# FFN gate and up projections: one 512-column product for the high weights, with the two sums in the halves of a PSUM bank

## What is computed

```
for i in range(DEPTH):                       # DEPTH = 2
    x = x + 0.5 * swiglu(rmsnorm(x, ffn1_norm[i]), ffn1_w_gate[i], ffn1_w_up[i], ffn1_w_down[i])
    ...                                      # mixer and memory attention
    x = x + 0.5 * swiglu(rmsnorm(x, ffn2_norm[i]), ffn2_w_gate[i], ffn2_w_up[i], ffn2_w_down[i])
```

## Time and profile before

| | us |
|---|---|
| median of 3 runs | 2211.28 |
| lowest and highest | 2208.55, 2211.59 |
| the profiled execution | 2215.75 |
| its span, first to last instruction | 2214.0 |
| PE busy in the span | 1791.3 |
| DVE, ACT busy in the span | 806.9, 594.3 |

### The profile page before, as it was taken

The page is one execution under the profiler, slowest core; times in us unless marked ns, Lnnn a source line. Parts: engine busy times, 40 slices in busy tenths (PEclk is TensorE's granted clock), DMA queues, the critical chain, the costliest instruction groups (busy, mean ns, idle before and its releaser), DMA issues.

```text
span 2214.0 us, 29558 instructions
## 1 busy us (share of the span) xinstructions
PE 1791.3 (81%) x12664; PEld 1299.1 (59%) x12664; DVE 806.9 (36%) x925; ACT 594.3 (27%) x691; POOL 142.7 (6%) x131
## 2 busy tenths in 40 slices
PE   7999998999999998999998875656665666665655
PEld 7999986999999995799997721111111111111111
DVE  6557557666756655676566300000000000000001
ACT  5334555433533345443345100000000000000001
POOL 3100001400000000120000200000000000000000
PEclk9999999999999999899999788888788888878887
DMA  6555542455555643055556289999999999999996
GB/s 228 197 174 175 170 154 83 165 173 200 197 171 172 212 128 125 20 197 194 189 175 228 114 354 427 430 427 430 427 429 428 428 429 428 429 428 429 428 429 288
DMA packets 181330, 603.84 MB, mean 273 GB/s; under 512 B 11904, under 2 KB 139392, under 8 KB 156688
## 3 DMA queue, kind: packets, MB, share of 16 engines
q1 hardware_dynamic: 178928, 600.40, 69.8%
q10 hardware_dynamic: 2080, 1.96, 0.3%
q0 software_dynamic: 256, 0.52, 0.1%
HBM read 601.81 MB, written 1.05 MB: 272 GB/s over the span
## 4 chain that ended last, share of the span: by engine, by line
PE 53%; DMA 38%; DVE 5%; ACT 3%; issue 1%; SPq 0%; DVEq 0%; ACTq 0%
DMA bulk<-in_w_down 19%; PE ps L961 19%; DMA bulk<-in_w_up 18%; PE ps L973 11%; PE ps L1125 3%; PE ps L1448 2%; PE ps L1470 2%; PE ps L931 2%; PE ps L1026 1%; PE ps L1027 1%; PE ps L1028 1%; PE ps L1140 1%; DMA bulk<-in_ffn_w_up 1%; PE ps L1010 1%; PE ps L1036 1%; PE ps L1037 1%
## 5 line engine op out<-in xcount | busy, mean ns | idle before, releaser
L1448 PE MATMUL ps<-bulk 128*32 128x512 f32 x2048 | 314.6, 747 | 218.5 <-DMA bulk<-in_w_up 132.3
L961 PE MATMUL ps<-part,part 128*128 128x256 f32 x3840 | 460.6, 280 | 0.1
L961 PEld LDWEIGHTS ps<-part,part 128*128 128x128 f32 x3840 | 456.1, 188 | 0.7 <-DVE part L1984 0.4
L1448 PEld LDWEIGHTS ps<-bulk 128*32 128x32 f32 x2048 | 63.2, 123 | 460.2 <-issue 172.0
L1984 DVE TENSOR_TENSOR part<-bulk,part 128x2048 fp32r<-128x2048 f32 x88 | 202.8, 2346 | 253.8 <-ACT part L1531 253.0
L1470 PE MATMUL ps<-bulk 128*32 128x512 f32 x1024 | 173.7, 812 | 107.7 <-DMA bulk<-in_w_down 104.3
L973 PE MATMUL ps<-part,part 128*128 128x256 f32 x2112 | 255.4, 279 | 1.9 <-DVE keep L2096 1.1
L973 PEld LDWEIGHTS ps<-part,part 128*128 128x128 f32 x2112 | 251.6, 188 | 2.3 <-ACT keep L1607 1.3
L2494 DVE TENSOR_TENSOR bulk<-bulk,ps 128x512 f32<-128x512 f32 x16 | 11.0, 688 | 598.2 <-PE ps L1448 598.2
L1531 ACT ACTIVATE part<-bulk 128x2048 fp32r<-128x2048 f32 x86 | 160.2, 1911 | 255.2 <-DMA bulk<-in_ffn_w_up 240.8
L1470 PEld LDWEIGHTS ps<-bulk 128*32 128x32 f32 x1024 | 32.9, 129 | 231.3 <-DMA bulk<-in_w_down 158.0
(11 more groups left out here) (279 smaller groups left out, 2013.1 us busy)
## 6 DMA issues: line engine op xcount, KB each, us to landing
bulk<-in_w_gate SPq DMA_DIRECT2D x64, 2048.0 KB, 26.0
bulk<-in_w_up SPq DMA_DIRECT2D x64, 2048.0 KB, 26.1
bulk<-in_w_down SPq DMA_DIRECT2D x64, 2048.0 KB, 26.2
bulk<-in_ffn_w_gate SPq DMA_DIRECT2D x44, 1024.0 KB, 7.4
bulk<-in_ffn_w_up SPq DMA_DIRECT2D x44, 1024.0 KB, 9.9
bulk<-in_ffn_w_down SPq DMA_DIRECT2D x44, 1024.0 KB, 5.0
bulk<-in_w_out SPq DMA_DIRECT2D x16, 1024.0 KB, 4.9
bulk<-in_gla_w_in SPq DMA_DIRECT2D x14, 1024.0 KB, 5.1
```

The lines of the kernel that those rows point to most:

```text
L961: ins = pe.matmul(y, w_, x_, start=(k == m == 0), stop=(k == KD - 1 and m == 2))
L1448: ins = pe.matmul(ps[j * CAP:(j + 1) * CAP, half, :], xe[:, k, :], w[:, kk, j * HALF:(j + 1) * HALF], start=(k == 0), stop=(k == KD - 1))
```

## The change

The x of the FFN keeps its high and its low part at a fixed distance, and a view `x_both(k)` names both at once: two runs of 256 columns. One product now takes the high weights by these 512 columns into a whole bank: columns 0 to 255 are the high sum, columns 256 to 511 the product with low x. The product of low weights and high x (256 columns) is added to the high half. Bank 2j + i now holds half j of projection i (gate, up), so a chunk takes banks 0 to 3, and there is room for one chunk.

The two halves of a bank are added at the evacuation: ACT copies the low half of the two banks of half chunk j to SBUF (`second_part`), DVE adds the high half to it (`gu_sum`, which frees the two banks), and scales in a second instruction (`gu_scaled`), now from SBUF. gate_up(c) waits for the sum of half chunk 0 of chunk c - 1 before half 0, and for that of half chunk 1 before half 1. Chunk 0 of f = 0 is made as before, in 256-column products, and its sum is a copy.

```
-        gate_sb = ffnbuf[:, 0:4 * CW].rearrange("p (b j t) -> p b j t", b=2, j=2)
+        gu_sb = ffnbuf[:, 0:4 * CW].rearrange("p (j i t) -> p j i t", j=2, i=2)
...
+        def x_both(k):
+            return bass.AP(x_parts, k * T, [[x_parts.shape[1], P], [X_HI - X_LO, 2], [1, T]])
...
+                def gu_step(b, i, j, k):
+                    (w_h, _), _, (w_l, x_h) = terms(b, i, j, k)
+                    pe.matmul(bank(2 * j + i), w_h, x_both(k), start=(k == 0), stop=False,
+                              skip_group_check=True)
+                    return pe.matmul(ps[:, 2 * j + i, 0:T], w_l, x_h, start=False, stop=(k == KD - 1),
+                                     skip_group_check=True)
...
                 def gate_up(c, b):
-                    if not (isinstance(c, int) and c < 2):
-                        pe.wait_ge(gu_free, NCH * f + c - 1)
                     for j in range(2):
+                        pe.wait_ge(gu_free, (c + NCH * f) * 2 + j - 1)
                         for i in range(2):
                             if j == 0:
                                 pe.wait_ge(gu_split, (c + NCH * f) * 2 + i + 1)
-                            y = ps[:, 2 * b + j, i * T:(i + 1) * T]
                             for k in range(KD):
-                                for m, (w_, x_) in enumerate(terms(b, i, j, k)):
-                                    ins = pe.matmul(y, w_, x_, start=(k == m == 0), stop=(k == KD - 1 and m == 2))
-                    ins.then_inc(gu_used, 1)
+                                ins = gu_step(b, i, j, k)
+                        ins.then_inc((gu_first, gu_used)[j], 1)
...
+                def second_part(c, j):
+                    act.wait_ge((gu_first, gu_used)[j], c + NCH * f + 1)
+                    act.wait_ge(gu_free, (c + NCH * f) * 2 + j)
+                    act.activation(lo_sb, ps[:, 2 * j:2 * j + 2, T:2 * T], ACT.Copy).then_inc(gu_second, 1)
...
                 def chunk(c, b, gu=True, dn=True):
-                    act.wait_ge(ga_done, c + NCH * f + 1)
-                    act.activation(gate_sb[:, b], gate_sb[:, b], ACT.Silu).then_inc(gate_done, 1)
+                    if not (isinstance(c, int) and c == 0):
+                        second_part(c, 0)
+                        second_part(c, 1)
+                    act.wait_ge(ga_done, (c + NCH * f) * 2 + 2)
+                    act.activation(gu_sb[:, :, 0, :], gu_sb[:, :, 0, :], ACT.Silu).then_inc(gate_done, 1)
...
+                def gu_sum(c, j):
...
+                        dve.wait_ge(gu_second, (c + NCH * f) * 2 + j - 1)
+                        if j == 0:
+                            dve.wait_ge(hid_ready, c + NCH * f)
+                        ins = dve.tensor_tensor(gu_sb[:, j], ps[:, 2 * j:2 * j + 2, 0:T], lo_sb, ALU.add)
+                    ins.then_inc(gu_free, 1)
+
+                def gu_scaled(c, j):
+                    r2 = rrow.unsqueeze(1).broadcast_to([P, 2, T])
+                    dve.wait_ge(gu_free, (c + NCH * f) * 2 + j + 1)
+                    dve.tensor_tensor(gu_sb[:, j], gu_sb[:, j], r2, ALU.mult).then_inc(ga_done, 1)
...
                 def chunk(c, b, gu=True, dn=True):
-                    r2 = rrow.unsqueeze(1).broadcast_to([P, 2, T])
-                    dve.wait_ge(gu_used, c + NCH * f + 1)
-                    dve.tensor_tensor(gate_sb[:, b], ps[:, 2 * b:2 * b + 2, 0:T], r2, ALU.mult).then_inc(ga_done, 1)
-                    dve.tensor_tensor(up_sb, ps[:, 2 * b:2 * b + 2, T:2 * T], r2, ALU.mult).then_inc(gu_free, 1)
-                    dve.wait_ge(gu_free, c + NCH * f + 1)
+                    for j in range(2):
+                        if not (isinstance(c, int) and c == 0):
+                            gu_sum(c, j)
+                        gu_scaled(c, j)
```

More of the change, by code:

```diff
@@ L193, in hi @@
             at = (bulk_at if ap.tensor.name == bulk.name else keep_at) + 4 * ap.offset
+            if n == KD * T and (at - bulk_at) // 4 in (X_LO, X_HI):
+                return bass.AP(x_parts, (at - bulk_at) // 4 - X_LO, [[x_parts.shape[1], P]] + [list(d) for d in ap.ap[1:]])
             key = (at, n)
@@ L249, in program @@
         ga_done = sem("ga_done")
+        gu_first = sem("gu_first")
+        gu_second = sem("gu_second")
         gu_free = sem("gu_free")
@@ L923, in gate_up_first @@
                         pe.wait_ge(gu_split, NCH * f * 2 + 2)
[L924 to L927, removed]
+                    if f:
+                        for j, k in [(j, k) for k in range(KD - 3) for j in range(2)] + [(j, k) for j in range(2)
+                                                                                           for k in range(KD - 3, KD)]:
+                            if j == 0 and k % 2 == 0:
+                                fed(n, k // 2)
                             for i in range(2):
-                                y = ps[:, 2 * b + j, i * T:(i + 1) * T]
-                                for m, (w_, x_) in enumerate(terms(b, i, j, k)):
-                                    ins = pe.matmul(y, w_, x_, start=(k == i == m == 0), stop=(k == KD - 1 and m == 2),
-                                                    skip_group_check=True)
+                                ins = gu_step(b, i, j, k)
+                            if j == 0 and k == KD - 1:
+                                ins.then_inc(gu_first, 1)
                     for m in range(0 if f else 3):
@@ L935, in gate_up_first @@
                             pe.wait_ge((gu_hi, gu_hi, gu_split)[m], i + 1)
-                            for k in range(KD):
-                                if i == 0 and k % 2 == 0:
+                            for j, k in ([(j, k) for k in range(KD) for j in range(2)] if m < 2 else
+                                         [(j, k) for j in range(2) for k in range(KD)]):
+                                if i == j == 0 and k % 2 == 0:
                                     if m == 0:
@@ L941, in gate_up_first @@
                                         fed(n, k // 2)
[L942 to L945, removed]
+                                w_, x_ = terms(b, i, j, k)[m]
+                                ins = pe.matmul(ps[:, 2 * j + i, 0:T], w_, x_, start=(k == m == 0),
+                                                stop=(k == KD - 1 and m == 2), skip_group_check=True)
+                                if i == 1 and j == 0 and k == KD - 1 and m == 2:
+                                    ins.then_inc(gu_first, 1)
                     ins.then_inc(gu_used, 1)
@@ L2040, in ffn @@
                 q = 1 - p
+                def gu_sum(c, j):
+                    if isinstance(c, int) and f == c == 0:
+                        dve.wait_ge((gu_first, gu_used)[j], 1)
+                        ins = dve.tensor_copy(gu_sb[:, j], ps[:, 2 * j:2 * j + 2, 0:T])
+                    else:
+                        dve.wait_ge(gu_second, (c + NCH * f) * 2 + j - 1)
[7 more added lines that the diff above has]
+                    dve.tensor_tensor(gu_sb[:, j], gu_sb[:, j], r2, ALU.mult).then_inc(ga_done, 1)
                 split_gu(f, 1, q)
+                gu_sum(0, 0)
+                gu_sum(0, 1)
                 split_dn(f, 0, p)
```

22 lines of the change are left out of this document (15 added, 7 removed).

## The result

The changed kernel takes 2312.9 us (median of four runs, 2310.2 to 2319.5), the kernel before 2211.2 us beside it. The ratio is 1.0467, 95% interval 1.0443 to 1.0491: 101.7 us slower. The forecast was 2300 us, 13 us too low; the sign, the new wait and the slow clock were right, the gain from the products was not. The profiled run is the slowest of the four, 2319.5 us, 6.6 above the median; its span is 103.6 us longer than that of before.

A forecast was written before the change was run, and what follows sets the result against it. PE was taken to bound the FFNs. Waits 80.5 + slow clock 28.9 - products 18.9 - 1.9 absorbed = +88.6 us, on the median 2211.3 giving 2300 us; range 2262 to 2330.

The forecast's parts named there:

- The bound: Inside the four FFNs PE waits for nobody (0.1 us idle), so each us lost or won there counts in full.
- The new wait: gate_up(c+1) waits for DVE's sum of chunk c, queued behind splits; neighbouring waits sum to 4.2 us, 80.5 in all.
- D + 20.7: When DVE's sum of half chunk 0 would end, in us after the end of down(c-2); PE there at 16.5.
- The products: In gate_up a 512-column product takes 222 ns, a chunk saves 0.44 us, 43 chunks give back 18.9 us.
- rival C: In gate_up the 512-column product takes 235.6 ns, so a chunk stays at 16.96 us: +101, 2312 us; chance 0.12.
- The clock: After long FFN waits PE runs at 1.2 GHz, 1.5 us lost each, at about 19 of 36 gates: 28.9 us.
- the 1.9 called absorbed: The 1.9 us by which today's chunks 2 to 10 exceed 16.96 us, subtracted from the forecast sum.
- Rival A: In the FFNs the clock holds, or falls so late that little runs slow: +61, 2273 us; chance 0.20.
- rival B: In the FFNs the clock stays low longer, 3 us lost per long wait: +115, 2326 us; chance 0.08.
- Nothing for the evacuation: New ACT copies and DVE instructions per chunk cost nothing as work, since both engines idle over 6 us per chunk.
- asked for 11 us later: In each chunk down(c) needs the evacuated result only 11 us later, so the added evacuation work costs nothing.
- Rivals D and E: In the FFNs: DVE's chain 4.2 us shorter, no waits, 2192 us, 0.03; or 512-column product 427 ns, 2474 us, 0.01.

The follow-up runs named there:

- Experiment 2: The changed kernel with DVE's sum of half chunk 0 one place earlier, ahead of the down split: 2255.6 us, ratio 1.020.
- experiment 3: The changed kernel with ACT's copy and DVE's sum of half chunk 0 ahead of both splits: 2218.7 us, ratio 1.0038.
- experiment 7: The sum-first kernel with two more orders, its 512-column product varied: one stretch 2206.3, 16 weight columns 2206.6, zeros 2203.6 (bf16) and 2204.2, in rows 2208.1 and 2193.9 (bf16) us.
- experiment 6: The sum-first kernel with two more orders, each 512-column product replaced by two of 256: 2217.1 us, ratio 1.0032.
- experiment 5: The sum-first kernel with the down part earlier at an FFN's start and the lambda work moved into DVE's idle time: 2208.6 us, ratio 0.9994.

## Why the prediction was right, and where it was off

**The bound.** Right: the FFNs ran at PE's pace, and each microsecond of waiting there came out at the end.

**The new wait.** Right in place, cause and pattern. The sum was to end at D + 20.7 and PE to be there at D + 16.5; it was 20.65 and 16.85 (112.48 + 16.85 = 129.33, 48 products after 123.69). Two neighbouring waits sum to 3.8 us, in the pattern of 0 and 3.8 that the slow clock was to make of it. Experiment 2 took 2.3 us from the chain and 2.3 from each pair; experiment 3 took the loads out of it and the waits for half chunk 0 went. Per FFN: 17.7, 14.9, 15.5, 20.7 us, forecast 20.0, 21.5, 18.0, 22.4; in sum 68.8 against 82, or 80.5 once the slow clock is counted in. The profile's idle time is short by 0.16 us at each wait, since a product of 256 columns is recorded as 0.28 us long and the next could start after 0.12: so 3.62 us of idling stand for a wait of 3.8, and 68.8 for 72.0. Most of the rest of the difference follows from PE's later arrival; in f = 1 the 4.4 us before down took the place of another part.

**The products: the term that was mis-sized.** "I take 222 ns, near per product": this is the step that failed. The 11 ns by which today's 256-column step exceeded 106.7 belong to the columns: 256 take 118 ns and 512 take 232. A gate_up went from 11.3 to 11.2 us, not to 10.86, and the 43 chunks gave back 4.3 us where 18.9 were counted. The end at 235.6 ns, rival C, was the near one. That its 2312 us is what was measured is in part luck: its waits and its slow clock were too short by some 3 and 4 us, and it gave the products no gain where 4.3 us were measured. From the 16-column row it followed rightly that little is the load of the weights (experiment 7 agrees), and that the rest is a price per product or per column; between these two I chose without a row that tells them apart, since all rows had one length. The Trainium skill, "TensorE: Matmul & The Clock Gate", section "Back-to-back issue gap", gives N/2.4 + 2.5 ns for a single product's gap, 215.8 for 512 columns: the bf16 products here agree (216), the fp32r ones do not (118 and 232). For a stream of weight loads and products it gives some 131 ns at 512 columns, and no row here is near that.

**The clock.** Right in kind and near in size: the steps in the FFNs that are longer than 118 or 233 ns without being waits sum to 32.9 us, in the kernel before to 1.5, so 31.4 against a forecast of 28.9 less the 1.9 called absorbed, 27.0. There were 17 slow stretches, forecast 19, several of them longer than the 1.5 us assumed. The granted clock over the FFN stretches was 0.94 to 0.96, not some 0.90. Rival A falls with it, and rival B, 3 us at each, is what happened at some gates only.

**Nothing for the evacuation.** Right within some 2 us: experiment 6 has it all, with the old number of products, and its FFNs, from each one's first down to its last, sum to 682.7 us by PE's time line, in the kernel before to 680.5.

**What was missed:** the late sums push the first hid of f = 1 back, behind the start of a long GpSimd instruction. The down part was said to be asked for 11 us later, and that was taken for cover; at an FFN's start there is none. In the kernel before, the hid of chunk 0 was ready 5.4 us before PE asked for it:

```profile
416.15 0.69 DVE L2058 TENSOR_TENSOR part<-keep,part 128x512 fp32r<-128x512 f32 x1
...
422.26 5.82 PE L973 MATMUL ps<-part,part 128*128 128x256 f32 x48
```

The two sums, which wait for ACT's copies, and the down split behind them used up some 4.5 us of that. The multiplication and the cast, each beside an instruction of GpSimd, took 1.65 and 4.61 us in place of 0.69 and 0.52, 5.1 more in all, and PE waited 4.4.

**The sum again**, for the profiled run: waits 68.8 + 4.4, slow clock 31.4, products -4.3 make +100.3 of the 103.6 us. The 0.16 us that the idle time leaves out at each of the 21 waits, 3.4 in all, is the rest. Against the forecast of +88.6 the products are 14.6 us worse, the waits with down (76.6 against 80.5) 3.9 better, the clock (31.4 against 27.0) 4.4 worse: 15.1 of the 15.0 by which the profiled span exceeds its forecast. So the total came nearer than the worst of its terms, with one error set off against another.

**Rivals D and E.** No wait disappeared by itself; the long product took 232 ns, not 427.

## What to carry to other kernels

When a change makes PE wait for an evacuation, look at what stands ahead of that evacuation in the other engine's queue, not at how long it takes: 0.7 us of vector work in each chunk, queued behind splits that hang on a load, cost 102 us here, in waits and in the slow clock after them; in front of the splits 8 us were left, and with two more orders put right nothing that can be measured. Where an engine's queue holds work for two clients, the step that frees a buffer goes first, and short work of DVE that PE waits for is kept clear in time of long instructions of GpSimd: let these meet work that has room. Before merging products to save a fixed price per product, measure the step at both lengths: if it is a price per column, there is nothing to save, and a price per product is not shown by one length.

## What the runs showed of the hardware

- **A column of fp32r costs 0.45 ns, one of bf16 0.42**, at 2.4 GHz: steps of 118 and 232 ns at 256 and 512 columns, in turns, in a row, with one stretch or two, with 16 or 128 columns of weights, with zeros or data; 216 ns for 512 columns in bf16, measured with zeros. At 1.2 GHz the excess is gone: from 212.09 to 212.52 and to 212.74 in the changed kernel, 0.43 and 0.22 us, 512 and 256 columns at 1.2 GHz being 0.427 and 0.213. A fixed number of clocks more per column would have made these 0.46 and 0.24 us (232 and 118 ns doubled). So something with a time of its own limits fp32r; which, no run here shows.
- **A cast of DVE stood still beside a GpSimd instruction**: 4.61 and 4.60 us in place of 0.52, ending 0.28 us after it, and 0.53 once it ran before it. By the Trainium skill, "SBUF — State Buffer", section "SBUF: two separate sides", DVE and GpSimd share a pair of ports; of a GpSimd instruction and a DVE one that uses both its ports or has two inputs in SBUF, the one that starts first holds the pair to its end, and the other is blocked. The rows agree, also those of the two splits and of GpSimd's own 6.58 us in experiment 5; that the cast is of the kind that uses both ports, no run here shows by itself.
- **The clock did not fall at every wait.** In the FFNs of the changed kernel it fell at every wait of 2.9 us or more except one of 3.6 us (172.27); in experiment 2 it held after all waits of up to 2.2 us and fell after those of 3.0 and 4.4.
